# One decoder layer in fp32: the seams from the norm to attention reordered, the last projection pair split by token halves, two weight slabs split on GpSimd

## The reference, cut to what matters

```python
n = rmsnorm(h, g_mix); z = n @ w_in                        # 1024 tokens x 1024 channels
qa, ka, va, qi, ki, wi, cq, ckv, kr, ga, gb = split(z)
y_a = dsa_attention(qa, ka, va, qi, ki, wi * idx_scale, positions, topk=256)  # indexer scores pick the keys
q_b = rmsnorm(cq, g_cq) @ w_uq; kv = rmsnorm(ckv, g_ckv) @ w_ukv              # then rope, causal attention -> y_b
h = h + (sigmoid(ga) * (y_a @ w_pa) + sigmoid(gb) * (y_b @ w_pb)) @ w_out
h = h + square(relu(rmsnorm(h, g_mlp) @ w_ff1)) @ w_ff2
h = h + sigmoid(rmsnorm(h, g_ple) @ w_ple_gate) * (p @ w_ple)
out = rmsnorm(h, g_final)
```

## Time and profile before

| | |
|---|---|
| median of three runs | 1735.89 us (1733.52 to 1736.64) |
| the profiled execution: its own time / its span | 1734.33 us / 1732.5 us |
| busy share of the span | PE 95%, PE weight loads 74%, DVE 68%, ACT 40%, POOL 37% |
| chain that ended last | PE 84%, DVE 8%, ACT 3%, issue 2%, DMA 2%, POOL 1% |
| granted TensorE clock, mean | 0.982 of 2.4 GHz |

### The profile page before, as it was taken

The page is one execution under the profiler, slowest core; times in us unless marked ns, Lnnn a source line. Parts: engine busy times, 40 slices in busy tenths (PEclk is TensorE's granted clock), DMA queues, the critical chain, the costliest instruction groups (busy, mean ns, idle before and its releaser), DMA issues.

```text
span 1732.5 us, 22637 instructions
## 1 busy us (share of the span) xinstructions
PE 1645.8 (95%) x8344; PEld 1287.3 (74%) x8344; DVE 1171.8 (68%) x1826; ACT 690.0 (40%) x1139; POOL 636.1 (37%) x397
## 2 busy tenths in 40 slices
PE   5899989999999999999999899999999999999997
PEld 4658778787755666667888777888878888888786
DVE  7349999990335566655434766776689999998335
ACT  5342232322255566651124433434354444444223
POOL 2212342221210000022211544445479888886221
PEclk9999999999999999999999999999999999999999
DMA  5201113224300010002443143344387445521112
GB/s 156 82 21 35 55 49 97 87 96 119 78 1 1 2 51 24 2 1 73 146 158 133 49 157 135 134 166 169 134 287 272 159 143 176 180 86 61 43 55 97
DMA packets 110342, 171.92 MB, mean 99 GB/s; under 512 B 18752, under 2 KB 68928, under 8 KB 110240
## 3 DMA queue, kind: packets, MB, share of 16 engines
q1 hardware_dynamic: 106400, 156.93, 27.3%
q10 hardware_dynamic: 3680, 13.63, 2.1%
q0 software_dynamic: 160, 0.02, 0.0%
HBM read 121.14 MB, written 47.58 MB: 97 GB/s over the span
## 4 chain that ended last, share of the span: by engine, by line
PE 84%; DVE 8%; ACT 3%; issue 2%; DMA 2%; POOL 1%; SPq 0%; ACTq 0%; DVEq 0%; POOLq 0%
PE ps L2064 34%; PE ps L2451 16%; PE ps L2410 14%; PE ps L2295 3%; PE ps L2309 3%; PE ps L2260 2%; PE ps L2279 2%; PE ps L2266 2%; PE ps L2174 2%; PE ps L2122 2%; PE ps L2135 1%; DMA hid_scratch<-t_out 1%; PE ps L2374 1%; DVE prob_a L1737 1%; PE ps L2236 1%
## 5 line engine op out<-in xcount | busy, mean ns | idle before, releaser
L947 POOL TENSOR_TENSOR w_lo<-w_raw,w_hi 128x1024 fp32r<-128x1024 f32 x67 | 165.7, 2475 | 526.8 <-ACT w_hi L1096 526.8
L1015 POOL TENSOR_TENSOR a_lo<-s_raw,a_hi 128x512 fp32r<-128x512 f32 x128 | 188.5, 1480 | 94.9 <-ACT a_hi L1339 94.0
L1096 ACT ACTIVATE w_hi<-w_raw 128x1024 fp32r<-128x1024 f32 x67 | 70.8, 1060 | 358.6 <-PE ps L2064 311.6
L2064 PE MATMUL ps<-n_hi,w_hi 128*128 128x512 f32 x576 | 181.6, 397 | 17.1 <-POOL w_lo L947 4.6
L2410 PE MATMUL ps<-b_hi,a_hi 128*128 128x512 f32 x448 | 177.3, 396 | 10.2 <-ACT u_two L1397 4.4
L2064 PE MATMUL ps<-n_lo,w_hi 128*128 128x512 f32 x576 | 180.0, 394 | 0.0
L2064 PE MATMUL ps<-n_hi,w_lo 128*128 128x512 f32 x576 | 180.0, 394 | 0.0
L2451 PE MATMUL ps<-b_hi,a_hi 128*128 128x512 f32 x448 | 174.4, 389 | 2.4 <-DVE h L1957 2.4
L2410 PE MATMUL ps<-b_lo,a_hi 128*128 128x512 f32 x448 | 175.9, 393 | 0.0
L2410 PE MATMUL ps<-b_hi,a_lo 128*128 128x512 f32 x448 | 175.9, 393 | 0.0
L1015 POOL TENSOR_TENSOR a_lo<-f_raw,a_hi 128x512 fp32r<-128x512 f32 x96 | 137.0, 1441 | 105.6 <-ACT a_hi L1339 105.5
(11 more groups left out here) (314 smaller groups left out, 3141.9 us busy)
## 6 DMA issues: line engine op xcount, KB each, us to landing
f_raw<-in_w_ff_dram SPq DMA_DIRECT2D x64, 512.0 KB, 4.5
b_lo<-hid_scratch SPq DMA_DIRECT2D x112, 256.0 KB, 5.5
hid_scratch<-c_out SPq DMA_DIRECT2D x32, 512.0 KB, 5.0
w_raw<-in_w_in_dram SPq DMA_DIRECT2D x28, 512.0 KB, 3.6
hid_scratch<-t_out SPq DMA_DIRECT2D x15, 768.0 KB, 6.9
gates_scratch<-stage ACTq DMA_DIRECT2D x16, 512.0 KB, 2.7
sig_ab<-gates_scratch SPq DMA_DIRECT2D x8, 1024.0 KB, 6.0
x_tok<-in_x_dram SPq DMA_DIRECT2D x8, 512.0 KB, 10.2
```

The source lines that it names most:

```text
L947: pool.tensor_tensor(lo_of(first)[:, :, :], w_raw[s][:, :, :], hi_of(first)[:, :, :].bitcast(F32), ALU.subtract).then_inc(lo_ready, 1)
L1015: pool.tensor_tensor(slot(a_lo, o), first_of(o), slot(a_hi, o).bitcast(F32), ALU.subtract).then_inc(a_lo_done, 1)
L1096: act.activation(hi_of(first)[:, :, :], w_raw[s][:, :, :], ACT.Copy).then_inc(hi_ready, 1)
L2064: last = pe.matmul(bank(4 * half + 2 * j + t)[0:w, :], wm, xm[:, t * HALF:(t + 1) * HALF], start=(n == 0 and a), stop=(n == total - 1 and ...
```

## The change

Eight edits; the rest of the program is as before.
1. SP loads the first two slabs behind token tiles 4 and 5, no longer behind all eight and the positions. POOL makes both their high and low parts; ACT only counts them.
2. Token tiles 4 to 7 are turned into banks 4 to 7 (`x_bank`), tiles 0 to 3 as before into banks 0, 1 and 4, 5. So tile 4 waits for the reader of tile 3. `qi` is done in two token halves, the first with its first channel tile ahead of the transposes of token tile 7, and both slabs are held until the second half has used them.
3. ACT makes the high part of slab 2 ahead of its first sine and copies `qi` ahead of its second; DVE instead of ACT copies the rows with `wi` and `kr`; ACT makes the high part of slab 5 behind the `ki` copy.
4. Two of the sixteen `qa` steps come ahead of the turning of `wi`, twelve at units 2, 3, 5, 6 and so on to 17, 18, and two behind unit 19.
5. The transposes of `va` move from a group of their own into the free half of the `ckv` tile 1 group; `cq` tile 2 with `ckv` tile 0 follows directly on `cq` tiles 0 and 1. POOL makes the low part of the first gate slab between the low part and the sum of `cq` tile 2.
6. The first key group goes slab by slab, and waits for the second slab only when it comes to it. Of the last four value copies DVE makes two. A group without work keeps the order of the halves.
7. The order at the end is gate 1, feed 0, gate 2, feed 1, feed 2, gate 3, feed 3.
8. Gate 3 (product with the norm, sigmoid) and feed 3 (matmuls, product, sum) go by token halves.

```diff
-        VA_GROUP = TT + 6
-        SUM_GROUP = VA_GROUP + 3 + GATES_N
+        KA_GROUP = TT + 4
+        VA_GROUP = KA_GROUP + 3
+        SUM_GROUP = VA_GROUP + 1 + GATES_N
...
-        LATENT_GROUPS = ["q_rope", "q_nope", "swap_q", "q_nope", "k_nope", "k_nope", "v", "v"]
+        LATENT_GROUPS = ["q_rope", "q_nope", "swap_q", "q_nope", "k_nope", "k_nope", "v", "v", "none"]
...
+        def x_bank(t):
+            return bank(4 * (t % 2) if t < X_WHOLE else 4 + 2 * (t % 2), 2)
...
+        QA_AT = [u for u in range(2, len(IDX_UNITS)) if u % 3 != 1][:2 * DT - 4]
...
+                if t == TT - 4:
+                    load(wt(wi, 0, KT, QI0, WCOL))
+                if t == TT - 3:
+                    load(wt(wi, KT, KT, QI0, WCOL))
             sp.dma_start(pos_i[:, :], positions[0].partition_broadcast(P)).then_inc(pos_loaded, 16)
-            load_kn(wi, QI0)
...
+                if q == 2 * OUT_N - 1:
+                    load_feed(q - 1)
                 load_kn(pg, q * WCOL)
-                load_feed(q - 1)
-            load_feed(2 * OUT_N - 1)
...
-            lo_parts(2)
+            for _ in range(2):
+                s, first, num, filled = at_.slab()
+                pool.wait_ge(raw_loaded[s], filled)
+                pool.tensor_copy(hi_of(first)[:, :, :], w_raw[s][:, :, :]).then_inc(hi_ready, 1)
+                pool.wait_ge(hi_ready, num + 1)
+                pool.tensor_tensor(lo_of(first)[:, :, :], w_raw[s][:, :, :], hi_of(first)[:, :, :].bitcast(F32),
+                                   ALU.subtract).then_inc(lo_ready, 1)
...
-            def latent_lo(c):
+            def latent_lo(c, slabs=0):
                 full, dst_lo, dst_hi, total, first, before = LATENTS[c][0:6]
                 pool.wait_ge(c_hi, c + 1)
                 pool.tensor_tensor(dst_lo, full, dst_hi.bitcast(F32), ALU.subtract).then_inc(c_lo, 1)
+                lo_parts(slabs)
...
-            latent_lo(2)
+            latent_lo(2, 1)
             latent_lo(3)
-            lo_parts(2)
+            lo_parts(1)
             latent_lo(4)
...
-            hi_parts(2)
+                if TT - 3 <= t < TT - 1:
+                    ahead.slab()
...
+            hi_parts(1, 2)
             act.wait_ge(rope_arg, 1)
             link(act.activation(rope_r[lo:hi, :], rope_r[lo:hi, :], ACT.Sin))
             act.dma_start(rope_d[0], rope_r[lo:hi, :]).then_inc(rope_saved, 16)
             hi_parts(1, 2)
+            half = group(2)
+            act.activation(qi[:, :, :].rearrange("q a n -> q (a n)"), bank(4 * half, 4), ACT.Copy).then_inc(
+                psum_free[half], 1)
             act.wait_ge(rope_arg, 2)
             link(act.activation(stage[lo:hi, :], stage[lo:hi, :], ACT.Sin, scale=inv_c[lo:hi, 1:2]))
             act.dma_start(rope_d[1], stage[lo:hi, :]).then_inc(rope_saved, 16)
-            hi_parts(1, 2)
-            half = group(2)
-            act.activation(qi[:, :, :].rearrange("q a n -> q (a n)"), bank(4 * half, 4), ACT.Copy).then_inc(
-                psum_free[half], 1)
-            hi_parts(2)
+            hi_parts(1)
             half = group(2)
             act.activation(ki[0:HEAD_DIM, :], tile_ps(half, 0)[0:HEAD_DIM, :], ACT.Copy).then_inc(idx_ready, 1)
-            act.activation(ki_wi[HEAD_DIM:P, :], tile_ps(half, 0)[HEAD_DIM:P, :], ACT.Copy).then_inc(ki_out, 1)
+            act.wait_ge(idx_ready, 1)
             act.wait_ge(ki_out, 1)
             act.sem_inc(psum_free[half], 1)
+            hi_parts(1)
...
-            latent(4, tile_ps(half, 0), half)
-            latent_hi(4, half)
+            latent(4, tile_ps(half, 0), None)
+            latent_hi(4, None)
+            act.activation(va[:, :, :].rearrange("q t n -> q (t n)"), tile_ps(half, 1), ACT.Copy).then_inc(
+                psum_free[half], 1)
...
-                for j in range(4):
+                for j in range(4 if g == 0 else 2):
                     t = 4 * g + j
                     last = act.activation(vb[:, t, :], bank(4 * half + j), ACT.Copy, scale=kv_norm[:, t:t + 1])
-                last.then_inc(psum_free[half], 1)
+                if g == 0:
+                    last.then_inc(psum_free[half], 1)
+                else:
+                    last.then_inc(vb_act, 1)
+                    act.wait_ge(vb_act, 1)
+                    act.wait_ge(vb_dve, 2)
+                    act.sem_inc(psum_free[half], 1)
+            act.sem_inc(psum_free[at_.group()[0]], 1)
+            at_.turns -= 1
...
+            q = 2 * OUT_N - 1
+            half, _, _, free = at_.group(2)
+            for j, part in enumerate((slice(0, HALF), slice(HALF, S))):
+                act.wait_ge(gate_in, q + 2 + j)
+                if j == 1:
+                    freed(act, half, free)
+                act.activation(tmp[:, q % 2, :, part], tmp[:, q % 2, :, part], ACT.Sigmoid).then_inc(gate_fn, 1)
...
+            at_.group(2)
+            half, done, _, _ = at_.group(2)
+            complete(dve, done)
+            dve.tensor_copy(ki_wi[HEAD_DIM:P, :], tile_ps(half, 0)[HEAD_DIM:P, :]).then_inc(ki_out, 1)
...
+            half = group(2)
+            for j in range(2, 4):
+                dve.tensor_scalar(vb[:, 4 + j, :], bank(4 * half + j), kv_norm[:, 4 + j:5 + j], None,
+                                  ALU.mult).then_inc(vb_dve, 1)
...
+                parts = [slice(0, S)] if q < 2 * OUT_N - 1 else [first, second]
+                for part in parts:
+                    for t in range(2):
+                        last = part.stop == S and t == 1
+                        dve.tensor_tensor(tmp[:, q % 2, t, part], tile_ps(half, t)[:, part], rms[:, part],
+                                          ALU.mult).then_inc(psum_free[half] if last else gate_in, 1)
...
+                            dve.wait_ge(feed_first, 1)
+                        else:
+                            complete(dve, done)
+                    dve.wait_ge(gate_fn, q + 1 + (part.start != 0))
...
+                        dve.tensor_tensor(gate[:, 0, :], gate[:, 0, :], tile_ps(half, 0)[:, part], ALU.mult).then_inc(fed, 1)
+                        ins = dve.tensor_tensor(gate[:, 1, :], gate[:, 1, :], tile_ps(half, 1)[:, part], ALU.mult)
...
+            take_gate(1)
+            take_feed(0)
+            take_gate(2)
+            take_feed(1)
+            take_feed(2)
+            take_gate(3)
+            take_feed(3)
...
+            def turn_x(t):
+                at_.group()
+                if t in (2, 3):
+                    freed(pe, t % 2, 1)
+                if t == X_WHOLE:
+                    freed(pe, 1, 2)
+                if t > X_WHOLE + 1:
+                    freed(pe, t % 2, t // 2)
                 pe.wait_ge(x_scaled, t + 1)
                 for k in range(DT):
-                    last = pe.transpose(bank(4 * half, 2)[:, k * P:(k + 1) * P], x_tok[:, t, k * P:(k + 1) * P],
-                                        ident[:, :])
+                    last = pe.transpose(x_bank(t)[:, k * P:(k + 1) * P], x_tok[:, t, k * P:(k + 1) * P], ident[:, :])
                 last.then_inc(turn_done, 1)
-            freed(pe, (TT - 1) % 2, TT // 2)
+            qi_slabs = [at_.slab() for _ in range(DT // KT)]
+            def qi_part(t, ks):
+                for k in ks:
+                    s, first, num, _ = qi_slabs[k // KT]
+                    if k % KT == 0:
+                        pe.wait_ge(lo_ready, num + 1)
+                    xh, xl = normed(k)
+                    for j in range(2):
+                        wh, wl = hi_of(first)[:, k % KT, j * P:(j + 1) * P], lo_of(first)[:, k % KT, j * P:(j + 1) * P]
+                        for wm, xm, a, z in ((wh, xh, True, False), (wh, xl, False, False), (wl, xh, False, True)):
+                            last = pe.matmul(bank(2 * j + t), wm, xm[:, t * HALF:(t + 1) * HALF],
+                                             start=k == 0 and a, stop=k == DT - 1 and z)
+                    if t == 1 and k % KT == KT - 1:
+                        last.then_inc(slab_used, 1)
+            for t in range(TT - 1):
+                turn_x(t)
             pe.wait_ge(inv_copied, 1)
-            project()
+            freed(pe, 0, 2)
+            freed(pe, 1, 2)
+            qi_part(0, range(0, 1))
+            turn_x(TT - 1)
+            qi_part(0, range(1, DT))
+            at_.group()
+            for half in range(2):
+                freed(pe, half, TT // 2)
+            qi_part(1, range(DT))
...
+            qa_step(0)
+            qa_step(1)
+            freed(pe, 1 - half, filled)
...
-                if 1 <= u <= 2 * DT:
-                    qa_step(u - 1)
+                if u in QA_AT:
+                    qa_step(2 + QA_AT.index(u))
+            qa_step(2 * DT - 2)
+            qa_step(2 * DT - 1)
             pe.wait_ge(rel_done, 2 * len(IDX_UNITS))
-            for _ in range(3):
+            for _ in range(4):
                 project()
             half = group()
-            freed(pe, VA_GROUP % 2, (VA_GROUP - 2) // 2 + 1)
```

(35 more changed lines are left out.)

76 lines of the change are left out of this document (39 added, 37 removed).

## The result

The changed kernel took 1693.67 us (median of four runs, 1688.64 to 1697.4), 1735.48 before it on the same chip: ratio 0.9762, 95% interval 0.9738 to 0.9786. Predicted were 1703, range 1697 to 1712. It is faster by more than was summed. The profiled execution is the slowest of the four: 1697.4, span 1695.6. So the *profiled pair* (the first profile of each kernel) differs by 36.9 in the span, the medians by 41.8.

The account below looks back on a forecast made before the run. PE was taken to bound the kernel, busy 95% of the span, so gains come from its idle stretches, slow clock and tail. 1.8 + 9.6 + 13.2 + 5.5 + 2.5 = 32.6 off 1735.89 gives 1703.3; range 1697 to 1712.

Parts of the forecast that it names:

- latents: Latent projections: both PE waits (4.2, 4.6) and the slow starts behind them go; 13.2 us gained, bounds 9.5 to 13.6.
- heads: Key and value heads before attention: shorter waits for the weight low part and `vb`; 5.5 us gained, bounds 4 to 8.
- end: Last gate and feed by token halves: final norm starts sooner behind PE; 2.5 us gained, bounds 1.5 to 2.8.
- without GpSimd's new order PE would wait 1.1: First gate slab in the latents: if POOL's sum (2.4) came first, PE would wait 1.1 us.
- rival of the slower side: Whole kernel, slower than forecast: slow clock stays, 1709 (0.22); latents' gain lost, 1716.5 (0.08); slow GpSimd copy, about 1741 (0.03).
- D: Gates: ACT or the search, its 16 us spare wrong, binds and the latents' 13.2 go; 1716.5 us, chance 0.08.
- Indexer: From `ki`'s end through the next projection: waits and slow clock go; 9.6 us gained, bounds 7 to 10.5.
- that and the steps behind them I put at 2.0 too much: Indexer units 0 and 1, 2.93 us though narrower, and the steps behind: low clock costs 2.0 us, removed.
- Norm: Start up to `ki`'s end: earlier `qi`, less GpSimd and DVE contention; 1.8 us gained, bounds 0.6 to 4.1.
- the 0.8 for the interlock: Norm stage: DVE's scalings wait for GpSimd's weight instructions; 0.8 us lost, from 0 to about 2.
- If the slow clock costs what it cost before: Norm stage: assuming unchanged slow-clock cost, `ki` ends 2.6 us earlier; up to 1.5 more if the clock rises sooner.
- rival B: More gained than counted: early clock rise +1.5, GpSimd and DVE interlocking +0.8, faster attention +2; 1699 us, chance 0.12.

Follow-up runs that it names:

- again_3: The changed kernel, unaltered, run and profiled once more; 1693.73 us, ratio 0.977 to the kernel before.
- before_1: The kernel before the change, unaltered, profiled a second time; 1733.55 us.
- again: The changed kernel, unaltered, run and profiled again; 1694.91 us, ratio 0.978 to the kernel before.
- act_splits: Against the changed kernel: ACT again makes the first two weight slabs' high parts, slabs loaded at their old place; 1698.83 us, ratio 0.9791.

## Why the prediction missed: the mechanisms held, terms of the sum were too small

The mechanisms stand. The stalls of the indexer, the latents, the keys and the end were each brought back by an edit of their own; the part of the value copies was not undone by itself. The sizes: latents 13.2 predicted, 14.2 (stage 13.7) measured; heads 5.5 predicted, 5.0 from `q` to attention in the profiled pair, of which the keys' order is 4.3 (4.5); end 2.5, 2.6. That without GpSimd's new order PE would wait 1.1 was 1.4. No rival of the slower side came: a GpSimd copy took 1.03, within the bounds of 0.95 and 2.33, and nothing was late at the gates (against D). The search ends 14.8 us before PE needs it (374.62 and 389.38), where 16 were summed.

What failed are terms of the sum, and what they left out:

*Indexer, 9.6, bounds 7 to 10.5.* The stage gained 9.6 and the next projection's slow clock 1.7 in the profiled pair, 11.3 together, outside the bounds. The stage's start was right (+4.25 for +4.3). The term "that and the steps behind them I put at 2.0 too much" was too small. I had read it off two shapes; the clock column of the stretch gives a better size, for the kernel before (columns: stretch, length, PE, PEld, DVE, ACT, POOL busy, granted clock, DMA):
```profile
70.00:90.00 20.00, 16.53 (x64) 9.48 (x66) 6.58 (x11) 7.74 (x15) 2.93 (x3) 0.83 0.25 73
```
and the changed one:
```profile
70.00:90.00 20.00, 18.99 (x85) 10.14 (x85) 9.87 (x14) 9.29 (x21) 2.39 (x4) 1.00 0.20 59
```
A mean of 0.83 over 20 us is 6.8 us at the 1.2 GHz level, so up to 3.4 us lost, not 2.0. The stage came out 1.7 shorter than summed (43.7 for 44.9 and 0.5): 0.5 of it is what was put for short waits, which did not grow (0.4 for a relu, as before), and 1.2 is left for the slow clock, that is 3.2 in place of 2.0. The column has to be checked against the matmuls' spacing: in the changed kernel's first profile it says 1.00 from 28 to 34 us, while six matmuls there run 0.43 apart; in `again_3` the same matmuls run as far apart, and it says 0.50 from 28 to 32.

*Norm, 1.8, bounds 0.6 to 4.1.* 2.7 in the profiled pair, 3.9 by the means: inside its bounds, but both of its terms were too cautious. `qi` was to start at 30.5, or 31.3 with the 0.8 for the interlock; it started at 31.01, 31.09, 30.19 and 30.14. The two longer scalings cost DVE 1.5 in the first profile, and `qi` only 0.5. "If the slow clock costs what it cost before" is the other: of the 144 matmuls only the 6 ahead of tile 7 ran long (0.36 to 0.43 apart), all others at 0.227. That lost 0.8 to 1.2 in place of 1.8, and the transposes of tile 7 took 0.87 to 1.54 for the 1.5 put. So of the 1.5 that rival B gave for an early rise of the clock 0.6 came in the profiled pair, and 0.9 to 1.6 in the other three profiles.

*Behind attention, counted as 0.* It had no bounds at all, and it moved by 1.0 in the profiled pair and by 4.2 in the means. Two profiles with the same matmuls behind the same stall (PE works 0.9 and 0.8 of the 4 us before them) show what moves, the first 16 us of the chain's 984 matmuls, in `before_1`:
```profile
1045.34:1049.34 4.00, 4.00 (x10) 3.13 (x11) 3.93 (x4) 0.89 (x2) 3.19 (x2) 0.50 0.21 36
1049.34:1053.34 4.00, 4.00 (x15) 3.19 (x14) 2.73 (x4) 1.12 (x2) 1.29 (x1) 0.74 0.99 308
1053.34:1061.34 8.00, 8.00 (x37) 6.63 (x36) 4.26 (x5) 2.79 (x5) 5.04 (x4) 1.00 0.47 192
```
and in `again_3`:
```profile
1007.06:1011.06 4.00, 4.00 (x18) 3.29 (x19) 3.93 (x4) 1.85 (x4) 3.22 (x2) 1.00 0.20 32
1011.06:1015.06 4.00, 4.00 (x19) 3.34 (x18) 3.93 (x5) 1.40 (x4) 1.32 (x2) 1.00 1.01 318
1015.06:1023.06 8.00, 8.00 (x37) 6.60 (x37) 3.17 (x6) 2.51 (x4) 5.00 (x4) 1.00 0.47 188
```
10 and 15 matmuls in 4 us against 18 and 19: the same stall left the engine at the low clock once and at the full one the other time. In the last 4 us before them the granted clock had already fallen to a mean of 0.90 in `before_1`, and was 1.00 in `again_3`. The second gate stage does so within one kernel (87.34 for 384 matmuls in the first profile, 88.96 in `again`).

*Attention itself*, too, was given nothing. It took 301.8 in all five profiles of the kernel before, and 301.3, 303.1, 299.0 and 299.0 in the four of the changed one. That is the rest of the 6.4 in the heads' row, and its size is as uncertain as that of the loops.

**What stays open.** Whether this gift of 4.2 is the change's or chance. For chance: the changed kernel's first profile had 839.4, near the kernel before; its variants, which are the same behind attention up to the last projections, had 834.2 to 840.1, and over all 15 profiles with the new code the mean is 837.2, which leaves 2.4. For the change: the short form of y (245.2) came in 7 of these 15 and in none of 5 of the kernel before. If the form had nothing to do with the kernel, five profiles drawn from the 20 would all be without it about once in 12; and y was singled out after the profiles were seen. The timed runs do not decide it: of 15 of the changed kernel 4 lie at 1688.1 to 1688.9 and 11 at 1693.2 to 1697.9; of 34 of the kernel before on those chips and one more, 6 lie at 1730.8 to 1731.5 and the others at 1732.9 to 1736.6. The waits of PE behind attention are the same in both forms (`ACT u_two` 3.4 to 4.4 in all), and not ordered by form. The profiles of the kernel before are few, and were not made on each of the chips on which the short form was seen. Over all these runs the gain is 40.4 by the means and 39.5 by the medians; so some 1.4 to 2.3 of the first measurement's 41.8 was its four draws.

The range failed with it. Its low end, 1697, is all the parts at their upper bounds together (4.1 + 10.5 + 13.6 + 8 + 2.8 = 39.0), and the profiled pair, with 36.9, lies inside. What went beyond it is the indexer, over its own bound by 0.8, and the stages counted as nothing, which were given no width, though they alone moved by up to 6 us from profile to profile.

## What to carry to other kernels

Undo a stall in the estimate with all of its slow clock, and read that from the clock column of the stretch behind it, not from single shapes. Give the untouched stages a width as well: a stall in them may or may not be followed by the low clock, 1.6 to 2.8 us each time here, and a long kernel has several of them. Where GpSimd is given work beside a VectorE chain, look at how the two meet in more than one profile: free-running, the same code ended this stage at 64.1 to 69.2 us, by shifts of 0.1 to 0.3 us. Pinning it by a semaphore of that chain made the meeting repeat, but bought no measurable time.

## What the runs showed of the hardware

- A GpSimd copy of 128x1024 fp32 took 1.03 us where nothing stood in its way, the subtraction 2.35; the same instruction beside a VectorE one with two SBUF inputs took 2.03 and 3.2 to 3.4, and the VectorE scaling 1.28 alone, up to 3.46 beside GpSimd. The Trainium skill (SBUF — State Buffer, SBUF: two separate sides) says that whichever starts first holds the port for its whole length. The rows shown here agree but for one: at 16.70 and 16.73 DVE's record starts first by 0.03, and DVE's work still came second, so the profile's starts do not tell who won so close a race.
- The same idle stretch of 2.7 us (second gate stage) was followed by the low clock in some executions and not in others: the granted clock behind it stayed at 1.00 in the changed kernel's first profile and fell to 0.50 for 2 us in `again`. The Trainium skill (TensorE: Matmul & The Clock Gate, Part 1: The HAM clock gate) says that the number of slow matmuls at a kernel's start varies from run to run of one kernel. Here, behind a stall in the middle, it varies as well: 87.34 or 88.96 us for 384 matmuls.
- Stages in which PE never stands for more than about 1 us repeat closely: the 192.0 us of the latents came out at 191.96 to 192.02 in eleven profiles, on at least three chips, and at 191.83 in `act_splits`, whose code there is the same. So a change's effect in one stage can be read from single profiles far below what the timed total can tell.
